# Two heads per instruction and a Softplus in the stick-breaking attention, another issue order in the dilated attention

## The chip, the cores and the metric

The kernel runs on one core of a Trainium2 chip. The time is the device time of one execution in microseconds; lower is better. The kernel before takes 3784.22 us (median of three runs, 3783.95 to 3786.22). TensorE's clock has two levels, 1.2 and 2.4 GHz; the profile gives the granted clock as a share of the upper one.

## The reference, cut to what matters

One program computes two blocks, one after the other, for 256 tokens of width 1024 in float32. The first block (gated linear attention, latent attention, convolution, feed-forward, two layers) is not touched. The second block has two layers. Each is a norm, an attention, a feed-forward part and a gated addition. The attention of layer 0 is stick-breaking attention over 16 heads of 64, that of layer 1 is dilated attention over 8 heads with three dilations.

```python
def stick_breaking_attention(x, w_in, w_out):
    ...
        z = jnp.einsum('bqhd,bkhd->bhqk', q[:, t0:L], k[:, :L]).astype(jnp.float32) * scale
        ...
        past = s_idx < t_idx
        log_fail = jnp.where(past, jax.nn.log_sigmoid(-z), 0.0)
        later = lax.cumsum(log_fail, axis=3, reverse=True) - log_fail
        a = jnp.where(past, jnp.exp(jax.nn.log_sigmoid(z) + later), 0.0)
        outs.append(jnp.einsum('bhqk,bkhd->bqhd', a.astype(v.dtype), v[:, :L]))
    ...
def banded_attention(q, k, v, n_back):
    ...
    s = jnp.where(mask[None, :, None], s, -jnp.inf)
    lse = jax.nn.logsumexp(s, axis=-1)
    prob = jnp.exp(s - lse[..., None])
    o = jnp.einsum('nbhqk,nbkhd->nbqhd', prob.astype(v.dtype), v2)
```

log_sigmoid(-z) is minus softplus(z), and the exponent log_sigmoid(z) + later is z minus the sum of softplus(z) over this key and all later past keys. The dilated attention is a softmax over the three dilations' scores together, weighted sums of the values included.

## The kernel before, in words

All activations lie transposed in SBUF, features on the 128 partitions and tokens along the free dimension. Weights stream through a ring of three buffers of 1 MB that SyncE fills. A planner (`Plan`) gives every output tile a PSUM bank in the order in which TensorE will write it (`pl.tiles`, `pl.gemm`; `pl.on` chooses the banks that are taken in turn), and each engine's program waits for counters: `done(t)` (TensorE has written tile t), `freed(t)` (its reader has emptied the bank). `start_tile` waits until the bank's last user has been read. On ScalarE and VectorE every program is a written list, in order.

Stick stage (layer 0 of the second block). Queries, keys (`QK`) and values (`V2`) are ready. For one head the three causal blocks of 128 x 128 (keys in the partitions) lie side by side as 384 columns. Per head h: TensorE writes the logits (`sz`, L1111 and L1112, 64 rows, since a head is 64 wide). ScalarE copies them scaled (L1235), takes Abs and Exp (through `own`, L1242) and Ln (L1235). VectorE (`failures`) adds the positive part (L2243) and multiplies by the mask (L2244). TensorE sums over later keys with a triangular matrix (`sc`, L1124 to L1127). VectorE (`argument`) subtracts (L2253) and takes the minimum with 0 (L2255), ScalarE takes Exp, VectorE (`stick`) multiplies by the mask (L2260). After each second head TensorE multiplies with the values (`so`, L1136 to L1138), and VectorE copies the 128 rows of the pair to the operand of the output projection `b2out0` (L712), which waits for pair k before its k-th step. TensorE issues the logits of head h + 1 before the sums of head h. The buffers are parts of the temporaries `TA` and `TD`.

Dilated stage (layer 1). A unit u is one head and one half of the queries (u odd: both key tiles, so twice the work). TensorE writes the scores of the three dilations (`d.s`, L1160, 6 or 12 matmul records), VectorE adds the mask and takes the maximum (`dmax`, L2289, L2293, L2294), ScalarE takes Exp with the sum (`dexp`), VectorE inverts the sum and scales (L2309, L2310), TensorE transposes (`d.t`, L793, 3 or 6), ScalarE copies the transposes to SBUF, TensorE multiplies with the values (`d.v`, L1179, 6 or 12), VectorE copies the output (`dvalue`, L2301). TensorE's order is scores of u + 1, transposes of u, values of u. ScalarE's is copies of u, Exp of u + 1. VectorE's is maximum of u + 1, scaling of u, output of u - 1. Probabilities and transposes have one buffer each. A float32 matmul shows as two records; a transpose as one. The projection `b2out1` (L712) follows.

## Time and profile before

| | |
|---|---|
| median of the runs | 3784.22 us |
| profiled execution, its own time | 3782.29 us |
| its span | 3780.5 us |
| TensorE busy | 3365.9 us (89%) |
| VectorE busy | 1420.6 us (38%) |
| ScalarE busy | 853.3 us (23%) |
| mean granted clock of TensorE | 0.93 |
| stick stage, first logits to projection | 2725.67 to 2846.91 us |
| dilated stage, first scores to projection | 3328.18 to 3461.53 us |

Engines: PE is TensorE's matmul part, PEld its weight loads, DVE is VectorE, ACT is ScalarE, POOL is GpSimd, SP is SyncE. Times in a timeline or chain are from the span's start. A wait in square brackets is the engine's idle time ahead of the instruction and what ended it. Busy time of overlapping matmuls is counted once.

### The profile page before, as it was taken

Reading aid. Unit: us, or ns where it says so; the run is one execution under the profiler, and the core shown is the slowest. Engines: PE = TensorE matmul, PEld = TensorE weight load, DVE = VectorE, ACT = ScalarE, POOL = GpSimd, SP = SyncE. Lnnn points to the kernel's source line nnn. Section 1 sums busy time; section 2 is a strip of 40 time slices with the busy share of each in tenths; the row PEclk is TensorE's granted clock in tenths of the full one; section 3 lists DMA queues with packets and bytes.
Section 4 is the critical chain, followed back from the end, with each engine's and each line's share of the span. In section 5 each row is a group of like instructions: output and inputs, shape, how many; then the busy total and the mean of one; then the engine's idle time right before and its main releaser. Section 6 shows DMA issues by size and latency. Waiting matters only on the chain.

```text
span 3780.5 us, 34902 instructions
## 1 busy us (share of the span) xinstructions
PE 3365.9 (89%) x14299; PEld 2397.9 (63%) x14299; DVE 1420.6 (38%) x2517; ACT 853.3 (23%) x1476; POOL 150.8 (4%) x125
## 2 busy tenths in 40 slices
PE   6987898999999699989888999898868998977998
PEld 3655544444444588436776678787757887755887
DVE  2267785232211588123579321542032102223102
ACT  4033210132221333013320332211262102112101
POOL 4000000000000244000000000000000000000000
PEclk9988899999999899999989999998958999966999
DMA  5212134323333132222223323344402553301453
GB/s 190 72 51 56 34 112 135 90 68 112 101 104 108 57 100 90 69 65 78 57 66 110 94 83 129 123 142 128 133 1 87 149 154 111 112 28 42 135 155 100
DMA packets 419421, 362.00 MB, mean 96 GB/s; under 512 B 20848, under 2 KB 392612, under 8 KB 419264
## 3 DMA queue, kind: packets, MB, share of 16 engines
q1 hardware_dynamic: 416928, 359.11, 30.8%
q8 instruction: 114, 1.87, 0.2%
q0 software_dynamic: 2336, 0.67, 0.1%
q14 instruction: 43, 0.35, 0.0%
HBM read 358.70 MB, written 1.05 MB: 95 GB/s over the span
## 4 chain that ended last, share of the span: by engine, by line
PE 77%; DVE 14%; ACT 4%; issue 2%; DMA 1%; POOL 1%; DVEq 0%; ACTq 0%; POOLq 0%
PE banks L712 24%; PE banks L770 12%; PE banks L752 12%; PE banks L687 6%; PE banks L734 5%; DVE conv_out L1954 4%; PE banks L786 3%; ACT L1235 2%; PE banks L1014 2%; PE banks L793 1%; PE banks L1005 1%; DVE gla_att L2016 1%; POOL vector_rows L650 1%; PE banks L955 1%; PE banks L938 1%
## 5 line engine op out<-in xcount | busy, mean ns | idle before, releaser
L712 PE MATMUL banks<-operand_a,wring 128*128 128x256 f32 (+1 forms) x3104 | 769.5, 411 | 44.2 <-DVE operand_a L1750 29.1
L712 PEld LDWEIGHTS banks<-operand_a,wring 128*128 128x128 f32 x3104 | 599.2, 193 | 214.0 <-issue 138.2
L1954 DVE SCALAR_TENSOR_TENSOR conv_out<-conv_in,vectors,conv_out 128x512 f32<-128x512 f32 (+1 forms) x464 | 286.8, 618 | 15.2
L770 PE MATMUL banks<-operand_a,wring 128*128 128x512 f32 (+1 forms) x768 | 263.9, 499 | 21.9 <-DMA wring<-in_w_in_dram 12.8
L770 PEld LDWEIGHTS banks<-operand_a,wring 128*128 128x128 f32 x768 | 146.0, 194 | 132.0 <-issue 98.0
L752 PE MATMUL banks<-ffn_h,wring 128*128 128x512 f32 (+1 forms) x704 | 227.4, 486 | 0.0
L752 PE MATMUL banks<-ff_h,wring 128*128 128x256 f32 x1024 | 221.3, 379 | 0.0
L752 PEld LDWEIGHTS banks<-ff_h,wring 128*128 128x128 f32 x1024 | 194.6, 190 | 26.5
L1005 PE MATMUL banks<-operand_a,wring 128*128 128x512 f32 (+1 forms) x512 | 182.9, 514 | 19.4 <-DVE conv_in L1972 19.4
L752 PEld LDWEIGHTS banks<-ffn_h,wring 128*128 128x128 f32 x704 | 133.8, 190 | 92.9 <-issue 83.5
L770 PE MATMUL banks<-operand_b,wring 128*128 128x512 f32 (+1 forms) x512 | 174.0, 497 | 17.0 <-DMA wring<-in_mla_wo_dram 6.0
L734 PE MATMUL banks<-wring,operand_a 128*128 128x256 f32 x832 | 180.3, 379 | 0.5 <-DVE tmp_dve L1837 0.5
L1235 ACT ACT_TABLE_LOAD x137 | 175.8, 1283 | 3.1 <-PEq L2347 0.7
L734 PEld LDWEIGHTS banks<-wring,operand_a 128*128 128x128 f32 x832 | 158.0, 190 | 22.8 <-issue 1.4
L687 PE MATMUL banks<-operand_a_hi,weights_hi 128*128 128x512 f32 x352 | 138.0, 392 | 29.9 <-POOL weights_lo L655 29.9
L655 POOL TENSOR_TENSOR weights_lo<-wring,weights_hi 128x1024 fp32r<-128x1024 f32 x44 | 108.9, 2476 | 1356.3 <-ACT weights_hi L1235 1356.3
L1005 PEld LDWEIGHTS banks<-operand_a,wring 128*128 128x128 f32 x512 | 102.4, 205 | 84.6 <-issue 76.6
L770 PEld LDWEIGHTS banks<-operand_b,wring 128*128 128x128 f32 x512 | 97.2, 193 | 84.6 <-issue 65.6
L687 PE MATMUL banks<-operand_a_lo,weights_hi 128*128 128x512 f32 x352 | 137.7, 391 | 0.0
L687 PE MATMUL banks<-operand_a_hi,weights_lo 128*128 128x512 f32 x352 | 137.7, 391 | 0.0
L1825 DVE SCALAR_TENSOR_TENSOR resid<-resid,tmp_act 128x512 f32<-128x512 f32 (+1 forms) x32 | 17.9, 559 | 283.1 <-ACT tmp_act L1315 283.1
L1787 DVE TENSOR_SCALAR gate_rank<-banks 128x256 f32<-128x256 f32 x10 | 4.2, 425 | 295.2 <-PE banks L786 295.2
(302 smaller groups left out, 4088.1 us busy)
## 6 DMA issues: line engine op xcount, KB each, us to landing
wring<-in_w_in_dram SPq DMA_DIRECT2D x52, 1024.0 KB, 5.3
wring<-in_w_ada_dram SPq DMA_DIRECT2D x48, 1024.0 KB, 6.5
wring<-in_ffn_wup_dram SPq DMA_DIRECT2D x44, 1024.0 KB, 5.1
wring<-in_w_ff_in_dram SPq DMA_DIRECT2D x32, 1024.0 KB, 5.5
wring<-in_w_ff_out_dram SPq DMA_DIRECT2D x32, 1024.0 KB, 5.6
wring<-in_ffn_wdown_dram SPq DMA_DIRECT2D x32, 704.0 KB, 4.5
wring<-in_w_in_dram SPq DMA_DIRECT2D x36, 512.0 KB, 5.2
wring<-in_w_in_dil_dram SPq DMA_DIRECT2D x18, 1024.0 KB, 5.0
```

The source lines that it names most:

```text
L650: pool.dma_start(VS[r % P:r % P + k, r // P, rep * w:rep * w + w], SRC[name][did:did + k, :]).then_inc(ev("rows_in"), 16)
L655: pool.tensor_tensor(WL[:, u % 2, :, :], w, WH[:, u % 2, :, :].bitcast(F32), ALU.subtract).then_inc(ev("w_lo"), 1)
L687: mm = pe.matmul(bank(t, 0, n), w[:, k, :], x[:, k, 0:n], start=first, stop=last)
L712: mm = pe.matmul(bank(t, 0, n), w[:, k, j * P:(j + 1) * P], opnd[:, k, 0:n], start=k == 0, stop=k == kt - 1)
L734: mm = pe.matmul(bank(t, j * 256, j * 256 + 256), AF[:, k, tok * P:(tok + 1) * P], w[:, k, :], start=k == 0, stop=k == KD - 1)
L752: mm = pe.matmul(bank(t, 0, n), w[:, k % per, :], opnd[:, k, 0:n], start=k == 0, stop=k == kt - 1)
L770: mm = pe.matmul(bank(t + j, 0, n), w[:, k, j * P:(j + 1) * P], (AF if gate else opnd)[:, k, 0:n], start=k == 0, stop=k == KD - 1)
L786: mm = pe.matmul(bank(t, 0, n), cn("ones"), src[:, m, 0:n], start=m == m0, stop=m == m1 - 1)
L1005: mm = pe.matmul(bank(t, 0, n), w[:, k, :], AF[:, k, 0:n], start=k == 0, stop=k == KD - 1)
L1014: mm = pe.matmul(bank(t + j, 0, n), w[:, k, j * P:(j + 1) * P], AF[:, k, 0:n], start=k == 0, stop=k == KD - 1)
L1235: act.activation(dst, src, f, **kw).then_inc(*inc)
L1954: own(stt(dst, src, w, dst, ALU.mult, ALU.add))
```

## The change

In the stick stage everything is done for a pair of heads at once, as instructions over 2 x 384 columns. The logits of a pair lie in two neighbouring banks (0 and 1, or 2 and 3), the sums of a pair in banks 4 and 5, the outputs in 6 or 7. VectorE copies the logits, scales them and adds a mask of 0 and -1e30 in one instruction; the mask constants are changed to these values. ScalarE takes one Softplus over the pair; there is no multiplication by a mask, since both Softplus and Exp of the masked entries are 0. TensorE's order is: logits of pairs 0 and 1, then for each p the sums of p, the values of p - 1, the logits of p + 2. ScalarE's is: Softplus of 0, then Softplus of p + 1, Exp of p. VectorE's is: logits of p + 1, argument of p, output of p - 1.

In the dilated stage probabilities and transposes get two buffers each. TensorE issues transposes of u, values of u - 1, scores of u + 2; ScalarE Exp of u + 1, copies of u; VectorE keeps maximum of u + 1, scaling of u, and copies the output of u - 2. The first block is unchanged.

```diff
-    strict = i[:, None] < i[None, :]
-    add("stick", np.concatenate([strict, np.ones((P, P)), strict], 1), 1)
+    future = np.where(i[:, None] < i[None, :], 0.0, NEG)
+    add("stick", np.concatenate([future, np.zeros((P, P)), future], 1), 1)
...
-    PD, PDT, _ = area(t_at, ("dil_probs", [P, 1, 768]), ("dil_probs_t", [P, 1, 768]))
+    ZS, _ = area(td_at - 8192, ("stick_z", [P, 2, 2, 384]))
+    LF, _ = area(td_at, ("stick_failures", [P, 2, 2, 384]))
+    XS, _ = area(t_at, ("stick_arg", [P, 2, 2, 384]))
+    PD, _ = area(t_at, ("dil_probs", [P, 2, 768]))
+    PDT, _ = area(base + KD * 4096, ("dil_probs_t", [P, 2, 768]))
...
+            logit_banks, sum_banks, out_banks = (0, 2), (4,), (6, 7)
...
+    def banks(t, n):
+
+        b = pl.tile_bank[t]
+        return PS[:, b:b + 2, 0:n]
...
```

TensorE, stick stage:

```diff
+                logits(0)
+                logits(1)
+                for p in range(9):
+                    if p < 8:
+                        t = F[f"sc{p}"]
                         start_tile(t)
+                        counter("failures", 1)(0)
+                        cum = banks(t, 384)
+                        for j in range(2):
+                            lf = LF[:, p % 2, j, :]
...
+                    if p:
+                        t = F[f"so{p - 1}"]
+                        start_tile(t)
+                        counter("stick_exp", 1)(0)
...
+                    if p + 2 < 8:
+                        logits(p + 2)
```

TensorE, dilated stage:

```diff
-                dscores(0)
-                for u in range(16):
-                    h, qt = u // 2, u % 2
-                    if u + 1 < 16:
-                        dscores(u + 1)
-                    counter("probs", 1)(0)
-                    for jt in range(qt + 1):
-                        turn(F[f"d.t{u}"] + jt, [PD[:, 0, jt * 384 + g * P:jt * 384 + (g + 1) * P] for g in range(3)])
...
+                dscores(0)
+                dscores(1)
+                for u in range(17):
+                    if u < 16:
+                        counter("probs", 1)(0)
+                        for jt in range(u % 2 + 1):
+                            turn(F[f"d.t{u}"] + jt,
+                                 [PD[:, u % 2, jt * 384 + g * P:jt * 384 + (g + 1) * P] for g in range(3)])
+                    if u:
+                        dvalues(u - 1)
+                    if u + 2 < 16:
+                        dscores(u + 2)
```

ScalarE, stick stage:

```diff
-                        op(z, bank(t, 0, 384), ACT.Copy, free(t), scale=0.125)
-                        act.wait_ge(*freed(t))
-                        own(w, z, ACT.Abs)
-                        own(w, w, ACT.Exp, scale=-1.0)
-                        op(w, w, ACT.Ln, (ev("stick_softplus"), 1), bias=1.0)
...
+                def softplus(p):
+                    act.wait_ge(*freed(F[f"sz{p}"]))
+                    if p >= 2:
+                        act.wait_ge(*done(F[f"sc{p - 2}"]))
+                    op(LF[:, p % 2, :, :], ZS[:, p % 2, :, :], ACT.Softplus, (ev("failures"), 1))
+
+                softplus(0)
+                for p in range(8):
+                    if p + 1 < 8:
+                        softplus(p + 1)
+                    act.wait_ge(ev("stick_arg"), p + 1)
+                    x = XS[:, p % 2, :, :]
+                    op(x, x, ACT.Exp, (ev("stick_exp"), 1))
```

ScalarE, dilated stage:

```diff
                 dexp(0)
                 for u in range(16):
+                    if u < 15:
+                        dexp(u + 1)
                     for jt in range(u % 2 + 1):
                         t = F[f"d.t{u}"] + jt
                         act.wait_ge(*done(t))
...
-                    if u < 15:
-                        dexp(u + 1)
```

VectorE, stick stage:

```diff
+                mask = cn("stick").unsqueeze(1).broadcast_to([P, 2, 384])
+
+                def logits(p):
+
+                    t = F[f"sz{p}"]
                     dve.wait_ge(*done(t))
+                    stt(ZS[:, p % 2, :, :], banks(t, 384), 0.125, mask, ALU.mult, ALU.add).then_inc(*free(t))
...
+                    tt(x, ZS[:, p % 2, :, :], banks(t, 384), ALU.subtract).then_inc(*free(t))
                     dve.wait_ge(*freed(t))
                     ts(x, x, 0.0, None, ALU.min).then_inc(ev("stick_arg"), 1)
...
+                logits(0)
+                for p in range(8):
+                    if p + 1 < 8:
+                        logits(p + 1)
+                    argument(p)
+                    if p:
+                        outputs(p - 1)
+                outputs(7)
```

VectorE, dilated stage:

```diff
-                    ts(PD[:, 0, 0:nk], PD[:, 0, 0:nk], ST[:, u % 2, 3:4], None, ALU.mult).then_inc(ev("probs"), 1)
-                    if u:
-                        dvalue(u - 1)
+                    ts(PD[:, u % 2, 0:nk], PD[:, u % 2, 0:nk], ST[:, u % 2, 3:4], None,
+                       ALU.mult).then_inc(ev("probs"), 1)
+                    if u >= 2:
+                        dvalue(u - 2)
+                dvalue(14)
                 dvalue(15)
```

## Rows read from the trace of the kernel before

**Rows 1.** Windows: busy us (records) of each engine, granted clock, DMA share, GB/s.
```profile
2725.00:2847.00 122.00, 71.47 (x289) 58.71 (x289) 44.36 (x87) 83.14 (x114) 0.00 (x0) 0.52 0.03 9
3328.00:3460.00 132.00, 86.62 (x358) 71.15 (x359) 40.83 (x103) 25.16 (x57) 0.00 (x0) 0.51 0.01 4
```
**Rows 2.** Chain that ended last, 2725 to 2847 us, shares by engine and line.
```profile
by line: ACT L1235 30.4%; ACT tmp_act L1242 13.8%; ACT tmp_act L1235 10.5%; PE banks L1111 7.2%; ACT tmp_dve L1235 6.5%; issue 6.2%; PE banks L1136 5.1%; PE banks L1138 4.8%; DVE tmp_dve L2260 3.7%; PE banks L1137 3.2%; PE banks L1112 2.7%;
```
**Rows 3.** The same chain in order of time (start us, us, what), stick stage.
```profile
2776.80 0.50 ACT tmp_act L1235
...
2791.57 0.50 ACT tmp_act L1235
```
**Rows 4.** Stick stage, ScalarE: groups (busy us, mean ns), then timeline (start, us).
```profile
L1235 ACT ACT_TABLE_LOAD x31 | 39.8, 1283 | 0.6
L1235 ACT ACTIVATE tmp_act<-tmp_act 128x384 f32<-128x384 f32 x16 | 8.4, 522 | 0.2
...
2780.25 1.28 ACT L1235 ACT_TABLE_LOAD   x1
2781.54 0.52 ACT L1235 ACTIVATE tmp_dve<-tmp_dve 128x384 f32<-128x384 f32 x1
```
**Rows 5.** Timeline of TensorE in the middle of the stick stage.
```profile
2789.89 1.22 PE L1111 MATMUL banks<-b_qk 64*128 64x256 f32 x2
...
2791.46 0.79 PE L1124 MATMUL banks<-tmp_dve,late_consts 128*128 128x128 f32 x2
...
2793.47 1.22 PE L1111 MATMUL banks<-b_qk 64*128 64x256 f32 x2
```
**Rows 6.** Timeline of TensorE at the start of the stick stage.
```profile
2725.67 0.71 PE L1111 MATMUL banks<-b_qk 64*128 64x256 f32 x4 [0.89 <-ACT b_v L1235]
...
2726.18 0.42 PE L1112 MATMUL banks<-b_qk 64*128 64x128 f32 x4
...
2732.70 0.77 PE L1124 MATMUL banks<-tmp_dve,late_consts 128*128 128x128 f32 x2 [6.10 <-DVE tmp_dve L2244]
```
**Rows 7.** Timeline of TensorE at the end of the stick stage.
```profile
2844.98 0.66 PE L1136 MATMUL banks<-tmp_dve,b_v 128*64 128x128 f32 x2 [2.28 <-DVE tmp_dve L2260]
...
2846.91 5.34 PE L712 MATMUL banks<-b_operand,wring 128*128 128x256 f32 x18
```
**Rows 8.** Dilated stage: groups of instructions that are 768 wide.
```profile
L2293 DVE TENSOR_REDUCE stats<-tmp_dve 128x1 f32<-128x768 f32 x8 | 7.6, 953 | 0.8
L1235 ACT ACTIVATE dil_probs<-tmp_dve,stats 128x768 f32<-128x768 f32 x8 | 7.4, 926 | 0.0
...
L2310 DVE TENSOR_SCALAR dil_probs<-dil_probs,stats 128x768 f32<-128x768 f32 x8 | 5.0, 621 | 0.3
```
**Rows 9.** Timeline, first block, full clock: matmuls of 128 columns.
```profile
1842.28 1.95 PE L889 MATMUL banks<-gla_e_more 128*128 128x128 f32 x16
```
**Rows 10.** Dilated stage: timeline, and one entry (3374.15) of the chain.
```profile
3333.20 0.90 PE L793 MATMUL banks<-consts,dil_probs 128*128 128x128 f32 x3 [2.79 <-DVE dil_probs L2310]
...
3374.15 1.54 PE banks L793 x6
...
3376.32 2.79 PE L1179 MATMUL banks<-dil_probs_t,b_v 128*64 128x128 f32 x12 [0.63 <-issue]
...
3379.04 2.93 PE L1160 MATMUL banks<-b_qk 64*128 64x128 f32 x12
...
3384.39 0.90 PE L793 MATMUL banks<-consts,dil_probs 128*128 128x128 f32 x3 [2.42 <-DVE dil_probs L2310]
...
3385.87 1.54 PE L1179 MATMUL banks<-dil_probs_t,b_v 128*64 128x128 f32 x6 [0.58 <-ACT dil_probs_t L1235]
```
**Rows 11.** Windows, columns as in rows 1, around and beside the stick stage.
```profile
2728.00:2732.00 4.00, 0.00 (x0) 0.00 (x0) 0.56 (x1) 3.93 (x6) 0.00 (x0) 0.74 0.28 96
2848.00:2852.00 4.00, 4.00 (x17) 3.42 (x16) 0.00 (x0) 0.14 (x1) 0.00 (x0) 0.83 0.00 0
2000.00:2020.00 20.00, 14.45 (x64) 11.83 (x65) 18.64 (x40) 1.89 (x4) 0.00 (x0) 1.00 0.33 105
```

More of the change, by code:

```diff
@@ L319, in branch_phase @@
                     after=ada_slot if name[2:] == "0" and (name != "co0" or h) else lambda: None)
-    def units(tag, n, s_tiles, t_tiles):
-        pl.tiles(f"{tag}.s0", s_tiles(0))
-        for u in range(n):
-            if u + 1 < n:
-                pl.tiles(f"{tag}.s{u + 1}", s_tiles(u + 1))
-            pl.tiles(f"{tag}.t{u}", t_tiles(u))
-            pl.tiles(f"{tag}.v{u}", 1)
     def ada_half(l, b, h):
@@ L1115, in _ @@
-                logits(0)
-                for h in range(16):
-                    if h < 15:
-                        logits(h + 1)
-                    t = F[f"sc{h}"]
-                    start_tile(t)
-                    counter("failures", 1)(0)
-                    lf = TD[:, h % 2, :]
-                    pe.matmul(bank(t, 0, P), cn("tri"), lf[:, 0:P], start=True, stop=True)
-                    pe.matmul(bank(t, P, 256), cn("tri"), lf[:, P:256], start=True, stop=False)
-                    pe.matmul(bank(t, P, 256), cn("ones"), lf[:, 256:384], start=False, stop=True)
-                    pe.matmul(bank(t, 256, 384), cn("tri"), lf[:, 256:384], start=True, stop=True).then_inc(*made(t))
-                    if h % 2:
-                        t = F[f"so{h // 2}"]
-                        start_tile(t)
-                        pe.wait_ge(ev("sticks"), h + 1)
-                        for hh in (h - 1, h):
-                            o = PS[64 * (hh % 2):64 * (hh % 2) + 64, pl.tile_bank[t], :]
-                            at_ = TD[:, 2 + hh % 2, :]
-                            vv = V2[:, :, hh * 64:hh * 64 + 64]
+                    z = banks(t, 384)
@@ L1139, in _ @@
                         mm.then_inc(*made(t))
+                    if p + 2 < 8:
+                        logits(p + 2)
                 cols("b2out0", KD, B2, SEQ, lambda k: pe.wait_ge(*freed(F[f"so{k}"])))
@@ L1677, in _ @@
                         act.wait_ge(*done(t))
-                        if u:
-                            act.wait_ge(*done(F[f"d.v{u - 1}"]))
-                        op(PDT[:, 0, jt * 384:(jt + 1) * 384], bank(t, 0, 384), ACT.Copy, free(t))
-                    if u < 15:
-                        dexp(u + 1)
+                        if u >= 2:
+                            act.wait_ge(*done(F[f"d.v{u - 2}"]))
+                        op(PDT[:, u % 2, jt * 384:(jt + 1) * 384], bank(t, 0, 384), ACT.Copy, free(t))
             post(f"b2out{l}", F[f"mpre{l}"])
@@ L2234, in _ @@
                 dve.wait_ge(ev("angles"), 1)
-                mask = cn("stick")
-                def failures(h):
-                    dve.wait_ge(ev("stick_softplus"), h + 1)
-                    z, w, lf = TA[:, h % 2, 0:384], TA[:, 2 + h % 2, 0:384], TD[:, h % 2, 0:384]
-                    if h >= 2:
-                        dve.wait_ge(*done(F[f"sc{h - 2}"]))
-                    own(stt(lf, z, 0.0, w, ALU.max, ALU.add))
-                    tt(lf, lf, mask, ALU.mult).then_inc(ev("failures"), 1)
@@ L2246, in argument, with logits @@
[L2246 to L2253 removed]
+                mask = cn("stick").unsqueeze(1).broadcast_to([P, 2, 384])
+                def logits(p):
+                    t = F[f"sz{p}"]
+                    dve.wait_ge(*done(t))
+                    stt(ZS[:, p % 2, :, :], banks(t, 384), 0.125, mask, ALU.mult, ALU.add).then_inc(*free(t))
@@ L2254, in argument @@
+                def argument(p):
+                    t = F[f"sc{p}"]
+                    x = XS[:, p % 2, :, :]
+                    dve.wait_ge(*done(t))
+                    if p >= 2:
+                        dve.wait_ge(*done(F[f"so{p - 2}"]))
+                    tt(x, ZS[:, p % 2, :, :], banks(t, 384), ALU.subtract).then_inc(*free(t))
                     dve.wait_ge(*freed(t))
                     ts(x, x, 0.0, None, ALU.min).then_inc(ev("stick_arg"), 1)
-                def stick(h):
-                    x = TD[:, 2 + h % 2, 0:384]
-                    dve.wait_ge(ev("stick_exp"), h + 1)
-                    tt(x, x, mask, ALU.mult).then_inc(ev("sticks"), 1)
-                    if h % 2:
-                        t = F[f"so{h // 2}"]
-                        dve.wait_ge(*done(t))
-                        if h == 1:
-                            dve.wait_ge(*done(pl.last("wout1")))
-                        dve.tensor_copy(B2[:, h // 2, :], bank(t, 0, SEQ)).then_inc(*free(t))
@@ L2268, in _, with outputs @@
-                failures(0)
-                for h in range(16):
-                    argument(h)
-                    if h < 15:
-                        failures(h + 1)
-                    stick(h)
+                def outputs(p):
+                    t = F[f"so{p}"]
+                    dve.wait_ge(*done(t))
+                    if p == 0:
+                        dve.wait_ge(*done(pl.last("wout1")))
+                    dve.tensor_copy(B2[:, p, :], bank(t, 0, SEQ)).then_inc(*free(t))
+                logits(0)
```

78 lines of the change are left out of this document (42 added, 36 removed).

## Prediction

> **What bounds the kernel now.** I read the windows view first, since the change touches only two stretches of the second block: the stick-breaking attention (2725.7 to 2846.9 us) and the dilated attention (3328.2 to 3461 us). The reader should see TensorE busy for 71 of 122 us in the one and 87 of 132 us in the other, at a mean granted clock of 0.52 and 0.51, and DMA at 1 to 3% [rows 1]. So neither stretch is bound by weights, and in both TensorE waits for somebody. The chain of waits says for whom. In the stick stretch the three ScalarE entries at its head hold over half of the path, with the ACT lines L1235 and L1242 in front [rows 2]; the groups by form show why: 31 table loads of 1283 ns, more than all of one kind of activation (16 of 522 ns) [rows 4]. The pattern repeats every pair of heads: from one first copy on ScalarE to the same copy one pair later is 2791.57 - 2776.80 = 14.77 us [rows 3], eight times. In the dilated stretch the path alternates between TensorE and VectorE: the transposes (L793) waited 2.42 us for the scaled probabilities, and the values (L1179) waited for the ScalarE copy of the transposes [rows 10].
>
> **Stick stage: ScalarE.** A head loses the copy out of PSUM, Abs, Exp, Ln and two of its table switches (Exp to Ln and back); a pair of heads now has one Softplus and one Exp, each 768 wide. A 384-wide activation takes 522 ns [rows 4], a 768-wide one with a per-partition bias and a running sum 926 ns [rows 8]; I take 0.9 us. No row shows Softplus. Its table may be in one set with Exp (no loads, below) or in another (a load before every activation, above). From a load's start to the activation behind it is 2781.54 - 2780.25 = 1.29 us [rows 4]. So ScalarE has 1.8 us per pair at the least and 2 x (1.30 + 0.90) = 4.4 us at the most. I take 4.4, since every Exp/Ln alternation of the kernel before has its load. Against the 14.77 us this is the main gain.
>
> Here the Trainium skill speaks against the change. "ScalarE: Activation LUTs" (What ACT_TABLE_LOAD costs) puts a switch at 1283 ns for the load and 1380 ns for a drain, 2.66 us in all, and its table of sets says to batch by set, which an order that alternates Softplus and Exp does not do. The trace agrees on the load and disagrees on the drain, since the activation started 1.29 us after the load began. By the page of the Trainium skill ScalarE would have 2 x (2.66 + 0.90) = 7.1 us per pair, by the rows 4.4.
>
> **Stick stage: VectorE.** Per pair it now has the scaled and masked copy of the logits, the subtraction, the minimum and one output copy. A 768-wide reduction took 0.953 us, a 768-wide scalar operation 0.621 us [rows 8]. That is about 1.0 + 1.0 + 0.6 + 0.4 = 3.0 us, beside other work. The multiplications by the mask go. The mask's new constants have the old size, and the buffers that move take no instruction.
>
> **Stick stage: TensorE.** The matmuls are the same, so what counts is the clock and the packing. At half clock the 8 matmul records of one head's sums took 2793.47 - 2791.46 = 2.01 us and the logits of one head 2791.46 - 2789.89 = 1.57 us [rows 5]; the values of a pair took 2846.91 - 2844.98 = 1.93 us [rows 7]. At full clock 16 records of 128 columns took 1.95 us [rows 9], that is 0.112 us from one to the next, and the first two heads' logits, issued back to back on different row groups, took 2726.60 - 2725.67 = 0.93 us together [rows 6]. A pair at full clock is 16 x 0.112 + 0.2 = 2.0 (sums), 1.0 (logits) and half of 1.93, about 1.1 (values): 4.1 us. A pair at half clock is 2 x 1.85 = 3.7, then 1.7 to 3.1 for the logits (packed as at the start, or not), and 1.93: 7.4 to 8.7 us.
>
> Which clock? In the kernel before, TensorE finished its first logits at 2726.6 and had nothing until 2732.7 [rows 6], because ScalarE needed two loads and four activations per head; the granted clock fell inside 2728 to 2732 and stayed at 1.2 GHz to 2849 [rows 1, 11]. With the change the first sums need one copy on VectorE (1.0) and one Softplus (0.9, its load done during the wait), so TensorE idles about 1 us instead of 6, and afterwards it is busy 4.1 of every 4.4 us. Elsewhere 2.4 GHz held through 20 us in which TensorE was busy for 14.45 [rows 11]. I take full clock.
>
> **Stick stage: the sum.** First logits at 2725.67, + 0.93, + 1.05 (VectorE), + 0.95 (ScalarE) = first sums at 2728.6. The first Exp runs at about 2732.3, after its subtraction, and ends at 2733.2; with a load the third Softplus ends at 2735.4. Five more pairs at 4.4 us bring the last Softplus to 2757.4. Then sums 2.0, subtraction and minimum 1.7, Exp 0.9, values 1.1: 2763.1. Before it was 2846.91 [rows 7]: 83.8 us saved. The output projection also starts at full clock; before it ran at half to about 2849.3 (0.83 of 2848 to 2852) [rows 11], which gives back 1.2 us. Together 85 us. If no loads are needed TensorE's 4.1 us bounds the pair, 2 us less; if TensorE's starts cost 0.3 us each as at half clock, 5 us more. Nothing stands behind the waits that were added: SyncE has the next weights in the ring already, and the single pair of banks for the sums is free 1.0 us after a sum, while TensorE has 2.1 us of other work.
>
> **Dilated stage.** The change issues the scores of unit u + 2 after the values of unit u - 1, and doubles the probabilities and their transposes. But VectorE's order is unchanged: maximum of u + 1, then scaling of u. The transposes of u wait for that scaling, and so for the scores of u + 1, which TensorE still issues right in front of those transposes. The loop scores, maximum, scaling, transposes, values stays serial; "two ahead" moves TensorE's issue only. What goes is the wait between transposes and values. Before, 6 transposes began at 3374.15 and the values at 3376.32: 2.17 us; 3 began at 3384.39 and the values at 3385.87: 1.48 us. Twelve values took 3379.04 - 3376.32 = 2.72 us to the next group, 0.16 more than 12 x 0.213 [rows 10]. With other values ready, transposes take 6 x 0.213 + 0.16 = 1.44 and 3 x 0.213 + 0.16 = 0.80. Saved 0.73 and 0.68, over 16 units 11 us. The copies and the Exp that change places on ScalarE are hidden by VectorE and by the values in between (about 1 us each); without that cover each copy costs its 0.5 us again, 12 us in all, and the gain is gone. I take the clock to stay low here: the hole of 2.79 us before the first transposes is unchanged, the clock fell around it, and it stayed at half speed for the stretch (mean 0.51) [rows 1, 10].
>
> **The sum.** 85 + 11 = 96 us off the profiled execution's 3782.3 us (span 3780.5) gives 3686. The median of the runs is 1.9 us higher: 3784.2 - 96 = 3688 us.
>
> **Rivals.**
> 1. TensorE stays at 1.2 GHz through the stick stage (against: the hole shrinks from 6 us to 1; for: it was never raised in this stage, though TensorE was busy for 71 of 122 us). A pair is then 7.4 to 8.7 us, 3.0 to 4.3 more than above, over some 7.5 pairs 23 to 32 us, and the projection starts slowly again, 1 us: 3712 to 3721.
> 2. A switch here costs twice the 1.30 us of the loads seen, as if the engine had to empty first. ScalarE then bounds with 2 x (2.6 + 0.9) = 7.0 us per pair, 2.6 us more in each of 7: 3706. This is the drain that the Trainium skill states in "ScalarE: Activation LUTs" (What ACT_TABLE_LOAD costs).
> 3. The dilated stage gives nothing back, since the freed wait reappears in front of the scaling: 3699.
> 4. The dilated stage really overlaps, so that TensorE's 87 us of work plus starts bound it: about 42 us instead of 11, 3657. Against it stands VectorE's order.
> 5. Slower: Softplus is a costly function. It enters once per pair on the chain of ScalarE. With 12 us gained elsewhere, the kernel gets slower by 0.2% (8 us) once 8 pairs lose 20 us, that is at a pair of 17.3 us: a Softplus of 17.3 - 2.6 - 0.9 = 13.8 us, fifteen times any activation of this width. At that point the time is 3792 us, and Softplus replaces Abs, Exp and Ln on the path of every pair (L1242 and L1235 above). Nothing in the trace is like it.
>
> **How the numbers follow.** Forecast 0.69 (its own range 3682 to 3697), rival 1 0.13, rival 2 0.05, rival 3 0.06, rival 4 0.03, rival 5 0.02 for slower, and 0.02 for a Softplus or a stall just big enough to leave the time as it was. The range reaches from 3676, below the no-load case, to 3716, into rival 1. About 0.2% is what a measurement of this kernel can tell from no change. Faster has 0.96, within 0.2% 0.02, slower 0.02.
>
> **What would show it.** In the profile after: table loads in the stick stretch (about 16, or 1 to 2), the granted clock there at 1.00, the pair's period near 4.4 us with ScalarE busy nearly throughout, the projection L712 starting 37 us after the first logits; in the dilated stretch the transposes still waiting over 2 us for VectorE's scaling, the values not waiting for ScalarE, a length of 122 us. A clock of 0.5 in the stick stretch, a Softplus over 1 us, or scores that run under VectorE's maximum would make it wrong.

## The result, and the profile after

The changed kernel takes 3672.2 us (median, 3667.6 to 3677.2) against 3785.2 us (3784.0 to 3787.7) in the same comparison: ratio 0.9701, 95% interval 0.9684 to 0.9718, or 113 us less. The forecast was 96 us less, 3688 us, with 3676 as the lower end of its range. The direction and the larger part were right, and the time lies 4 us below the range.

Three stretches of the profile after, in the windows view (columns as in rows 1). The first two are the stick stage and the dilated stage, each from the first matmul on its scores to the first of its output projection. The third is the first 4 us of the last projection.

```profile
2733.10:2770.10 37.00, 31.68 (x288) 27.85 (x288) 21.91 (x31) 31.27 (x30) 0.00 (x0) 1.00 0.09 29
...
3250.30:3359.20 108.90, 73.00 (x360) 60.45 (x360) 41.21 (x104) 26.60 (x57) 0.00 (x0) 0.69 0.02 5
...
3359.00:3363.00 4.00, 3.73 (x17) 3.34 (x18) 0.00 (x0) 0.66 (x3) 0.00 (x0) 1.00 0.00 0
```

The same cuts of the kernel before:

```profile
2725.70:2846.90 121.20, 71.34 (x288) 58.56 (x288) 44.36 (x87) 82.72 (x113) 0.00 (x0) 0.52 0.03 9
...
3328.20:3461.50 133.30, 87.44 (x360) 71.53 (x361) 41.13 (x104) 24.95 (x57) 0.00 (x0) 0.51 0.01 4
...
3461.00:3465.00 4.00, 3.47 (x8) 2.86 (x9) 0.17 (x1) 0.00 (x0) 0.00 (x0) 0.50 0.00 0
3465.00:3469.00 4.00, 4.00 (x15) 3.28 (x14) 0.00 (x0) 1.32 (x4) 0.00 (x0) 0.73 0.00 0
```

The stick stage went from 121.2 to 37.0 us at a granted clock of 1.00, 84 us less. The dilated stage went from 133.3 to 109.0 us, 24.4 less. In both kernels it has the same 360 matmul records, so the row splits the gain: TensorE's idle time fell from 45.9 to 35.9 us (10.0 less) and its busy time from 87.4 to 73.0 us (14.4 less). Nearly all of the second is a faster clock for the same matmuls; about 1 us of it is that two groups with no wait between them now overlap at their ends. The projection behind it no longer starts at half clock, which shortens the rest of the kernel by 2.8 us. The stretch between the two stages gave 1.2. The profiled spans differ by 105 us and the medians by 113, mainly because the untouched first block ended 7.5 us later in this execution (last section).

The dilated stage by groups of one shape (busy us, mean ns, idle us before them and who ended it), first after, then before:

```profile
L1196 PE MATMUL banks<-dil_probs_t,b_v 128*64 128x128 f32 x144 | 31.6, 398 | 0.0
L1183 PE MATMUL banks<-b_qk 64*128 64x128 f32 x144 | 25.1, 329 | 0.9 <-ACT b_v L1264 0.9
L809 PE MATMUL banks<-consts,dil_probs 128*128 128x128 f32 x72 | 18.4, 410 | 35.3 <-DVE dil_probs L2332 35.3
```

```profile
L1179 PE MATMUL banks<-dil_probs_t,b_v 128*64 128x128 f32 x144 | 34.7, 425 | 9.7 <-issue 5.0 <-ACT dil_probs_t L1235 4.6
L1160 PE MATMUL banks<-b_qk 64*128 64x128 f32 x144 | 34.2, 415 | 0.9 <-ACT b_v L1235 0.9
L793 PE MATMUL banks<-consts,dil_probs 128*128 128x128 f32 x72 | 19.5, 431 | 35.5 <-DVE dil_probs L2310 35.5
```

Two readings: the wait in front of the values went from 9.7 us to nothing, and the wait of the transposes for VectorE's scaling stayed at 35 us. "Two ahead" hides nothing more behind VectorE; what went is one wait, and the same matmuls became shorter.

### The profile page after: what moved, and what is told of

Read it like the earlier page. It is cut to its first block, busy times and chain, and to the rows that moved or that the text cites. A ratio compares the mean times of both kernels' runs of the same rounds, so it can differ in the third digit from the quotient of the medians.

```text
span 3675.4 us, 34722 instructions
## 1 busy us (share of the span) xinstructions
PE 3315.4 (90%) x14299; PEld 2356.7 (64%) x14299; DVE 1397.7 (38%) x2461; ACT 804.3 (22%) x1393; POOL 151.0 (4%) x125
## 4 chain that ended last, share of the span: by engine, by line
PE 80%; DVE 13%; issue 2%; ACT 2%; DMA 1%; POOL 1%; DVEq 0%; ACTq 0%; POOLq 0%
PE banks L728 24%; PE banks L786 13%; PE banks L768 12%; PE banks L703 7%; PE banks L750 5%; DVE conv_out L1980 4%; PE banks L802 3%; PE banks L1021 2%; PE banks L1030 2%; PE banks L809 1%; POOL vector_rows L666 1%; PE banks L971 1%; PE banks L1057 1%; DVE gla_att L2042 1%; PE banks L954 1%
## 5 line engine op out<-in xcount | busy, mean ns | idle before, releaser
L768 PEld LDWEIGHTS banks<-ffn_h,wring 128*128 128x128 f32 x704 | 133.8, 190 | 92.9 <-issue 83.5
L671 POOL TENSOR_TENSOR weights_lo<-wring,weights_hi 128x1024 fp32r<-128x1024 f32 x44 | 108.9, 2476 | 1363.1 <-ACT weights_hi L1264 1363.1
```

Of the source, the lines that this page charges most:

```text
L671: pool.tensor_tensor(WL[:, u % 2, :, :], w, WH[:, u % 2, :, :].bitcast(F32), ALU.subtract).then_inc(ev("w_lo"), 1)
L768: mm = pe.matmul(bank(t, 0, n), w[:, k % per, :], opnd[:, k, 0:n], start=k == 0, stop=k == kt - 1)
```

## The experiments

All were compared with the kernel before on the same chip, at 3785.2 to 3785.5 us. Lengths of a stage run from its first scores to its projection, in the profiled execution.

### The two halves alone

The first kernel is the changed one with the old loop, buffers and orders of all engines in the dilated stage (its core is shown); the second is the kernel before with the new ones.

```diff
-    PD, _ = area(t_at, ("dil_probs", [P, 2, 768]))
-    PDT, _ = area(base + KD * 4096, ("dil_probs_t", [P, 2, 768]))
+    PD, PDT, _ = area(t_at, ("dil_probs", [P, 1, 768]), ("dil_probs_t", [P, 1, 768]))
...
+                for u in range(16):
                     h, qt = u // 2, u % 2
+                    if u + 1 < 16:
+                        dscores(u + 1)
+                    counter("probs", 1)(0)
...
```

> The stick stage of the kernel after, the dilated stage exactly as before. Clock theory and its rival alike: stick stage 37 us (2733.14 to 2770.17 in the kernel after), dilated stage 133 us as before at a mean granted clock of 0.51, total 3785 - 85 = 3700 us. If the changed stick stage also helped the dilated stage (another phase of the clock), the dilated stage is shorter than 130 us here.

> The dilated stage of the kernel after, the stick stage as before. If the 24.4 us of the dilated stage (133.3 to 109.0) belong to its own new order: dilated stage 109 us at a mean granted clock near 0.7, total 3785 - 27 = 3758 us. If they hang on the stick stage: 122 us at a clock of 0.51, total 3774 us.

Measured: the stick half 3697.6 us (ratio 0.9765, 0.9748 to 0.9781), 87.7 less; the dilated half 3758.6 us (0.9930, 0.9915 to 0.9944), 26.7 less. Together 114.4 against the whole change's 113: they add up. The stick stage took 37.0 us in the one and 121.2 in the other, the dilated stage 133.8 and 108.9. So the missed term is the dilated half's own, and owes nothing to the faster stage ahead of it.

### The removed wait put back

```diff
+                    if u < 16:
+                        for jt in range(u % 2 + 1):
+                            pe.wait_ge(*freed(F[f"d.t{u}"] + jt))
                     if u:
                         dvalues(u - 1)
```

TensorE waits for ScalarE's copies of unit u again before it goes on to the values of u - 1; buffers and order stay as changed.

> The kernel after, except that TensorE waits for ScalarE's copies of the transposes of u before the values of u - 1. This puts back a gap of about 0.6 us between transposes and values, 16 times, 10 us at constant clock. Clock theory (the gain beyond 11 us is granted clock, which comes with transposes, values and scores following each other without a gap): the clock falls back to about 0.51, the dilated stage takes 131 us or more, the projection starts at half clock, total 3699 us. Rival (all of the gain is waits and buffers): the stage takes 109 + 10 = 119 us, total 3682 us.

Measured: 3693.1 us (0.9759, 0.9744 to 0.9773); the stage took 128.4 us, 19.4 more than in the changed kernel. The windows view of its dilated stage:

```profile
3245.80:3374.10 128.30, 82.60 (x360) 67.87 (x360) 41.23 (x104) 26.61 (x57) 0.00 (x0) 0.56 0.01 5
```

TensorE's idle time rose from 35.9 to 45.7 us, the 10 us that were put back. Its busy time for the same records rose by 9.6 us as well (about 1 us of that is the overlap at the ends, lost again). So 10 us of waiting cost 19 us, and the granted clock (0.56 for 0.69) carries most of the other half. The result lies between the two expectations, nearer to the clock theory. The clock did not fall to the 0.51 of the old loop: 5 us of busy time stay, for which this pair of runs shows no cause.

### Only work added to the old loop

The stick half alone (dilated stage 133.8 us, clock 0.51), with 8 matmuls per unit that nobody reads, between the next scores and the wait for the probabilities. They go into bank 7, which the plan keeps free by giving the stage's tiles banks 0 to 6 only:

```diff
                     if u + 1 < 16:
                         dscores(u + 1)
+                    for _ in range(8):
+                        pe.matmul(PS[:, 7, 0:P], cn("ones"), cn("ident"), start=True, stop=True)
                     counter("probs", 1)(0)
```

> The kernel with the new stick stage and the old dilated stage, in which TensorE gets eight matmuls of 128 columns (16 records, result read by nobody, in a bank that the stage leaves free) between the scores of u + 1 and the transposes of u, where it waited 2.2 to 2.4 us. Order and waits stay those of before, work is only added. Clock theory (the granted clock of this stage follows what TensorE does, and it alone is worth a large part): once the clock is up, the pair takes 17.06 us less half of its 9.6 us of matmuls, about 12.5 us, the stage about 103 us instead of 133.8 at a clock near 1.0, total 3697 - 30 - 3 = 3664 us. Rival (the clock is not moved by work that is put in, or is not what the stage is short of): the added records stick out of the holes by 16 x 0.213 - 2.3 = 1.1 us per unit at half clock, the stage takes 150 us, total 3715 us.

Measured: 3660.7 us (0.9668, 0.9654 to 0.9683), 37 us faster than the same kernel without the additions; the stage took 98.1 us. Its windows row, TensorE's timeline over one unit (start, duration, what, idle before it), and the values as a group:

```profile
3244.90:3343.00 98.10, 82.19 (x617) 71.35 (x617) 41.13 (x104) 24.13 (x57) 0.00 (x0) 0.98 0.02 6
```

```profile
3295.23 1.60 PE L1185 MATMUL banks<-b_qk 64*128 64x128 f32 x12
3296.76 2.05 PE L1195 MATMUL banks<-consts 128*128 128x128 f32 x16
3299.25 0.55 PE L811 MATMUL banks<-consts,dil_probs 128*128 128x128 f32 x3 [0.44 <-DVE dil_probs L2330]
3300.38 0.87 PE L1206 MATMUL banks<-dil_probs_t,b_v 128*64 128x128 f32 x6 [0.58 <-ACT dil_probs_t L1262]
```

```profile
L1206 PE MATMUL banks<-dil_probs_t,b_v 128*64 128x128 f32 x144 | 18.9, 277 | 10.1 <-ACT dil_probs_t L1262 10.1
```

Sixteen unread groups of 2.05 us (L1195) fill the old wait for the scaling. TensorE's idle time drops from 46 to 16 us, the clock is 0.98, and the real matmuls take little more than half the time: 82.2 us less 16 x 2.05 us leaves 49 us for what took 87.4 us. The added work hid inside the wait; what it brought is the clock. This is the plainest proof in the case. Orders and waits are the old ones, the values still wait 10.1 us for ScalarE's copies (9.7 before), and 36 us went from the stage. So the clock can be up without transposes, values and scores following each other without a gap.

### The same dilated work in two other orders

TensorE takes the values of u - 1 before the transposes of u (in the plan too):

```diff
+                    if u:
+                        dvalues(u - 1)
                     if u < 16:
                         counter("probs", 1)(0)
...
-                    if u:
-                        dvalues(u - 1)
```

> The kernel after with TensorE's order values of u - 1, transposes of u, scores of u + 2, and VectorE's order as it is. The values then run inside the hole in which TensorE waits for maximum and scaling. The serial loop is scores, maximum, scaling, transposes. At half clock TensorE bounds, 11.4 us per pair, 95 us in all, total 3658 us. At full clock 2.0 + 4.6 + 1.2 = 8 us per pair, 68 us in all, total 3630 us. If it is the gapless run of transposes, values and scores that raises the clock, it stays near 0.5 here; if it is the share of time in which TensorE is busy, it goes up.

VectorE takes the scaling of u + 1 ahead of the maximum of u + 2:

```diff
+                dmax(0)
+                dmax(1)
+                dscale(0)
+                for u in range(16):
+                    if u + 1 < 16:
+                        dscale(u + 1)
+                    if u + 2 < 16:
+                        dmax(u + 2)
+                    if u:
+                        dvalue(u - 1)
```

> The kernel after with VectorE's order in the dilated stage changed: the scaling of u + 1 comes ahead of the maximum of u + 2, so that the transposes of u + 1 no longer wait for the scores of u + 2. Theory that VectorE's order is what keeps the stage serial: TensorE no longer waits 2.2 to 2.4 us per unit; bound by TensorE at half clock 45 records x 0.213 + 6 starts = 11 us per pair, 95 us in all (total 3658), at full clock 7 us per pair, 60 to 70 us in all (total 3625 to 3635). Rival (the ScalarE copies or the banks are next in line): no shorter than 105 us, total 3668 or more.

Measured: values first 3638.7 us (0.9611, 0.9595 to 0.9627), stage 76.9 us. VectorE's order 3627.6 us (0.9583, 0.9569 to 0.9597), stage 64.9 us. The same cuts as before, first of the values-first kernel, then of the reordered VectorE:

```profile
3242.50:3319.30 76.80, 58.07 (x360) 48.15 (x360) 41.13 (x104) 26.08 (x57) 0.00 (x0) 0.83 0.02 8
```

```profile
3246.80:3311.70 64.90, 54.39 (x361) 45.89 (x361) 41.94 (x104) 24.25 (x57) 0.00 (x0) 0.87 0.03 9
```

Values first leave 18.7 us of idle time; the time lies between what was expected at half and at full clock. In the reordered VectorE, idle time is 10.5 us instead of 35.9 and busy time 54.4 instead of 73.0: the overlap itself brought 25 us and the clock that came with it 19. This is the prediction's rival 4. It did not happen in the change, for the reason that the prediction gave (VectorE's order), and it happens when that order is changed. One unit in its timeline:

```profile
3270.41 0.17 DVE L2328 RECIPROCAL stats<-stats 128x1 f32<-128x1 f32 x1 [0.77 <-ACT dil_probs L1264]
3270.61 0.62 DVE L2329 TENSOR_SCALAR dil_probs<-dil_probs,stats 128x768 f32<-128x768 f32 x1
...
3271.28 0.88 PE L809 MATMUL banks<-consts,dil_probs 128*128 128x128 f32 x6 [1.04 <-DVE dil_probs L2329]
```

These six transposes wait 1.04 us for the scaling, where in the changed kernel six wait 2.22 us, and VectorE now waits 0.77 us for ScalarE's Exp. All the waits of transposes for the scaling sum to 9.8 us in this stage, against 35.3.

### Scores three ahead, and a warm start

With the change's VectorE order, the wait can also go if TensorE issues the scores one unit earlier, so that the maximum finds them ready:

```diff
                 dscores(1)
+                dscores(2)
...
-                    if u + 2 < 16:
-                        dscores(u + 2)
+                    if u + 3 < 16:
+                        dscores(u + 3)
```

> The kernel after with the scores one unit further ahead: scores of 0, 1 and 2 first, then transposes of u, values of u - 1, scores of u + 3. VectorE's and ScalarE's orders stay. Theory (VectorE does maximum of u + 1 before scaling of u, so the scores of u + 1 must not stand right in front of the transposes of u): TensorE's hole of 2.2 to 2.4 us closes, ScalarE's Exp hides behind the next maximum too, VectorE at 6.2 to 6.5 us per pair bounds, stage 55 to 62 us with a start at half clock, total 3672 - 50 = 3622 us, some us under the order with early scaling (3627.6). Rival (banks or the copies of the transposes are next): stage over 75 us, total over 3640 us.

The second kernel adds 8 unread matmuls once, between the first scores and the first transposes:

```diff
                 dscores(2)
+                for _ in range(8):
+                    pe.matmul(PS[:, 7, 0:P], cn("ones"), cn("ident"), start=True, stop=True)
```

> The same, with eight matmuls (16 records) that nobody reads between the first scores and the first transposes, into a bank the stage leaves free. TensorE waits there 2.8 us, and the clock fell in it. If that hole is what brings the half-clock start (about 10 us of it in the kernel with early scaling), the clock stays at 1.0, and the stage is 3 to 7 us shorter than without them: total 3617 us. Rival (the clock falls anyway, or VectorE bounds so that it doesn't matter): no difference beyond 2 us.

Measured: 3620.9 us (0.9568, 0.9552 to 0.9584), stage 55.6 us; and 3615.4 us (0.9554, 0.9539 to 0.9568), stage 51.1 us. The start of the stage, windows of 4 us, first without and then with the added matmuls:

```profile
3252.00:3256.00 4.00, 4.00 (x19) 3.45 (x18) 3.14 (x9) 1.74 (x5) 0.00 (x0) 0.50 0.00 0
3256.00:3260.00 4.00, 4.00 (x18) 3.12 (x17) 1.92 (x6) 1.52 (x4) 0.00 (x0) 0.50 0.02 6
3260.00:3264.00 4.00, 4.00 (x25) 3.55 (x24) 1.79 (x6) 0.72 (x3) 0.00 (x0) 0.72 0.00 0
```

```profile
3252.00:3256.00 4.00, 3.53 (x29) 3.05 (x28) 3.83 (x11) 2.23 (x5) 0.00 (x0) 1.00 0.00 0
3256.00:3260.00 4.00, 3.88 (x31) 3.13 (x29) 3.72 (x11) 2.80 (x6) 0.00 (x0) 1.00 0.02 6
3260.00:3264.00 4.00, 4.00 (x32) 3.42 (x30) 3.14 (x8) 1.58 (x5) 0.00 (x0) 1.00 0.00 0
```

Without them TensorE works through at half clock for some 11 us after its first hole of 2.46 us; with them the hole is 0.47 us and the clock never falls. The profiled stage is 4.5 us shorter, the medians differ by 5.5 us. It is the shortest of all the runs: 170 us below the kernel before and 57 below the change. What now limits it is TensorE's own work, and not VectorE as was expected:

```profile
3248.50:3299.50 51.00, 48.98 (x376) 41.44 (x376) 40.87 (x104) 25.85 (x57) 0.00 (x0) 1.00 0.04 11
```

It is busy for 49.0 of 51.0 us, at full clock; VectorE for 40.9.

### The stick stage: what Softplus gave, and what the table loads cost

Pairs and the new order, but with the old functions (Abs, Exp, Ln and VectorE's maximum) in place of Softplus; VectorE's list gets that operation and takes the logits two pairs ahead:

```diff
-                    op(LF[:, p % 2, :, :], ZS[:, p % 2, :, :], ACT.Softplus, (ev("failures"), 1))
+                    w = LF[:, p % 2, :, :]
+                    own(w, ZS[:, p % 2, :, :], ACT.Abs)
+                    own(w, w, ACT.Exp, scale=-1.0)
+                    op(w, w, ACT.Ln, (ev("stick_softplus"), 1), bias=1.0)
```

> The kernel after, but Softplus is taken as before: Abs, Exp, Ln on ScalarE over the pair of heads (two table loads more often than none: Exp to Ln and back), then a VectorE operation for the positive part. Pairing and order stay. Theory that most of the gain is the pairing (each instruction and each load does two heads) with the overlap: ScalarE per pair 4 x 0.85 + 2 x 1.3 = 6.0 us against 14.77 before and 4.3 with Softplus; stage 8 + 8 x 6.0 + 3 = 58 us at full clock, total 3672 + 21 = 3693 us. At half clock (the first sums come only after two loads, 6 us in which TensorE idles as before): bound by TensorE, 7.4 us per pair, 70 us, total 3705 us. Rival (Softplus is the main part): the stage stays over 85 us, total over 3720 us.

Softplus in place of the Exp, so that no table changes (the attention's weights are then other numbers, at the same amount of work):

```diff
                     x = XS[:, p % 2, :, :]
-                    op(x, x, ACT.Exp, (ev("stick_exp"), 1))
+                    op(x, x, ACT.Softplus, (ev("stick_exp"), 1))
```

> The kernel after with Softplus in place of the stick stage's Exp, so that no table switches fall inside it; the weights of the attention are then other numbers. ScalarE per pair falls from 4.31 to 1.7 us. Theory that ScalarE with its two loads and TensorE are nearly level: TensorE bounds at 3.9 to 4.1 us per pair, the stage goes from 37.0 to 34 to 36 us, total 3670 us, hardly to be told from 3672. Rival (the loads were still the price of the stage): over 8 us less.

Measured: 3688.2 us (0.9742, 0.9727 to 0.9756), 5 us under the nearer expectation, stick stage 57.1 us at a clock of 0.82; and 3672.9 us (0.9701, 0.9686 to 0.9715), stick stage 34.5 us. ScalarE by groups in the stick stage of the changed kernel, of the one with the old functions, and of the one without switches:

```profile
L1264 ACT ACT_TABLE_LOAD x14 | 18.0, 1283 | 0.2
L1264 ACT ACTIVATE stick_arg<-stick_arg 128x768 f32<-128x768 f32 x8 | 6.7, 844 | 3.3 <-DVE stick_arg L2278 3.2
L1264 ACT ACTIVATE stick_failures<-stick_z 128x768 f32<-128x768 f32 x8 | 6.7, 843 | 1.1 <-DVE stick_z L2267 1.0
```

```profile
L1264 ACT ACT_TABLE_LOAD x15 | 19.2, 1283 | 0.3
...
L1271 ACT ACT_TABLE_LOAD x2 | 2.6, 1283 | 0.0
```

```profile
L1264 ACT ACTIVATE stick_arg<-stick_arg 128x768 f32<-128x768 f32 x8 | 6.8, 844 | 15.1 <-DVE stick_arg L2278 15.1
...
L1264 ACT ACT_TABLE_LOAD x1 | 1.3, 1283 | 0.0
```

Of the stage's 84 us, 64 come without Softplus: from two heads per instruction, the new order, and the copy and the mask in one VectorE operation, which these runs do not separate. Of the 31 loads 14 go with them, because a pair of heads shares its switches. Softplus brings the other 20; in the medians it is 16, since the same dilated stage took 105.8 us in this kernel and 109.0 in the changed one. The loads beside Softplus cost only 2.6 us in all, since without them TensorE's 3.9 us per pair (0.86 of logits, 1.98 of sums, 1.08 of values by its timeline) stands right behind ScalarE's 4.3. In the total, 3672.9 against 3672.2 us, that is not to be seen; the dilated stage was 1.3 us longer in that kernel. The page "ScalarE: Activation LUTs" of the Trainium skill (section Table sets: the hidden batching unit) has Exp and Ln together in one set, with one load for both; the trace disagrees, since with the old functions it shows 17 loads for 8 pairs.

### Does a hole at the start keep the clock down?

Five copies on ScalarE ahead of the first Softplus make TensorE's first wait as long as it was before:

```diff
+                act.wait_ge(*freed(F["sz0"]))
+                for _ in range(5):
+                    own(XS[:, 1, :, :], ZS[:, 0, :, :], ACT.Copy)
                 softplus(0)
```

> The kernel after, with five more copies of 768 on ScalarE (4.3 us) in front of the first Softplus. TensorE then idles about 5.5 us after the first logits instead of 1.4. Theory (the idle start is what took the clock in the kernel before): the clock falls to half at the start of the stage; it comes back once sums and logits follow each other, as in the kernel with the old functions (clock 1.00 again 17 us after the first logits); the stage takes 37 + 4.3 + 4 to 9 us = 45 to 50 us, total 3682 us. Rival 1 (once low, it stays low in this stage): 65 us, total 3700 us. Rival 2 (the clock doesn't fall): 41.4 us, total 3676 us.

Measured: 3680.5 us (0.9724, 0.9709 to 0.9738), stick stage 44.4 us, just under the 45 to 50 expected. Windows of 4 us from the hole on:

```profile
2732.00:2736.00 4.00, 0.00 (x0) 0.00 (x0) 0.45 (x1) 3.85 (x6) 0.00 (x0) 0.73 0.27 96
2736.00:2740.00 4.00, 1.74 (x8) 1.77 (x9) 0.00 (x0) 3.97 (x4) 0.00 (x0) 0.50 0.00 0
2740.00:2744.00 4.00, 4.00 (x20) 3.39 (x20) 1.85 (x3) 0.51 (x2) 0.00 (x0) 0.50 0.01 4
2744.00:2748.00 4.00, 4.00 (x38) 3.55 (x38) 2.64 (x5) 3.94 (x5) 0.00 (x0) 0.99 0.00 0
```

The clock falls in the hole of 7.0 us, which ends at 2738.26, and is back by 2744, within 6 us of work. The hole is 5.6 us longer than in the changed kernel, where 4.3 of copies were meant: the table load of 1.28 us, which ran during TensorE's first logits, now stands behind the copies. Of the 7.4 us that the stage grew, the longer hole is 5.6 and the slow clock the other 1.7. So a single hole as long as the old one of 6.1 us [rows 6] does not keep this stage at half speed. The kernel with the old functions agrees: a first hole of 6.7 us that ends at 2734.0, half clock to 2740, 0.55 to 2744, 1.00 in 2744 to 2748, and 0.90 over the rest of the stage. There ScalarE makes TensorE wait 0.6 to 2.1 us before the sums of every pair. What kept the old stage at 0.52 for 120 us is then likely its waits in every pair, which were more and longer (49.9 us of idle time in all, against 18.4); no run shows this for the stick stage by itself, with only work added to its old loop.

### The changed kernel again

No edit; the same code once more, beside the runs above.

> The kernel after once more, on the chip of the three kernels beside it. If its first profile (span 3675.4) was long only because the untouched first block ended 7.5 us later than in the kernel before, this one has the stick stage at 37.0 us, the dilated stage at 105 to 111 us (its clock follows no fixed pattern from run to run), and a total of 3667 to 3677 us.

Measured: 3673.6 us (0.9707, 0.9692 to 0.9721), stick stage 37.0 us, dilated stage 109.0 us at a clock of 0.69. The dilated gain beyond the 11 us was no accident of one execution.

## Why the prediction was right and where it was wrong

**Stick stage: right, term by term.** Forecast 37.4 us to the projection, measured 37.0. The forecast had 4.4 us per pair, bound by ScalarE. The timeline of the stage after, one Softplus between its two loads and the sums that wait for it:

```profile
2762.22 1.28 ACT L1264 ACT_TABLE_LOAD   x1
...
2763.51 0.84 ACT L1264 ACTIVATE stick_failures<-stick_z 128x768 f32<-128x768 f32 x1
...
2764.37 1.28 ACT L1264 ACT_TABLE_LOAD   x1
...
2764.50 0.46 PE L1143 MATMUL banks<-stick_failures,late_consts 128*128 128x128 f32 x2 [1.04 <-ACT stick_failures L1264]
```

The sums wait 1.04 us for the Softplus, and start 17.24 us after those of four pairs earlier, 4.31 per pair. Both activations took 0.84 us where 0.90 was taken, from load to activation 1.29 us as read [rows 4], and the first hole was 1.37 us where "about 1" stood. Clock 1.00: rival 1 did not happen. The upper end of the choice on Softplus's table (a load before each activation) was the right one, and its cost small.

**Rivals 2 and 5.** The price of a switch was the 1.29 us of the trace, not twice that. An estimate with the Trainium skill's drain ("ScalarE: Activation LUTs", What ACT_TABLE_LOAD costs) is 7 us per pair; the trace disagrees with 4.31. Softplus at 0.84 us is no costly function.

**Dilated stage: the mechanism right, the size wrong.** "The transposes still waiting over 2 us": 2.22 and 2.42 us after, 35.3 us in all. "The values not waiting for ScalarE": nothing instead of 9.7 us. Predicted 1.44 and 0.80 us from transposes to values:

```profile
3317.72 1.54 PE L809 MATMUL banks<-consts,dil_probs 128*128 128x128 f32 x6 [2.22 <-DVE dil_probs L2332]
...
3319.19 1.54 PE L1196 MATMUL banks<-dil_probs_t,b_v 128*64 128x128 f32 x6
...
3324.87 0.90 PE L809 MATMUL banks<-consts,dil_probs 128*128 128x128 f32 x3 [2.42 <-DVE dil_probs L2332]
...
3325.70 2.58 PE L1196 MATMUL banks<-dil_probs_t,b_v 128*64 128x128 f32 x12
```

Measured 1.47 and 0.83 us. Against 2.17 and 1.48 before that is 0.70 and 0.65 less, 10.8 us over 16 units: the 11 us are there. Rival 3 fell with that, and rival 4 did not happen.

**The step that failed** is "I take the clock to stay low here". The term was 11 us and measured 24.4 in the stage and 2.8 in the projection behind it. Of the 24.4, the removed wait is the 10.8 just given, and the other 13.6 are the same records at a mean clock of 0.69 in place of 0.51. With the projection's 2.8 that is the 16 us beyond the term. The reason given, that the hole of 2.79 us before the first transposes was unchanged, was no reason: the runs with a hole at the start show that the clock returns within 6 to 11 us if work follows, and the old loop with unread work runs at 0.98. What held the clock down was the waiting inside the units, and that was just what the change reduced. It was an omission in the range too: the stick stage had its rival on the clock, the dilated stage none, though it sat at 0.51 with the same kind of waits. All the matmuls of the stage at full clock would have been about 38 us less (87.4 to 49 us), so any part of the way up was worth several us, and the range should have gone below 3676 for it. That the loop would flicker instead of rising fully, no row of before could say.

What measure of the waiting decides stays open. TensorE's idle time in the stage was 45.9 us at a clock of 0.51 (before), 45.7 at 0.56 (wait put back), 35.9 at 0.69 (changed), 18.7 at 0.83 (values first), 15.9 at 0.98 (unread work) and 10.5 at 0.87 (VectorE reordered). The last two do not follow that order, and as a share of the stage the idle time hardly moved in the change itself: 34% before, 33% after. Less waiting came with more clock in the large, but no row gives a rule by which the 0.69 could have been forecast.

**The sum.** The stick half was put at 85 us and measured 87.7 (its stage 84.2, the rest small terms behind it that no run separates). The dilated half was put at 11 and measured 26.7. Of the 17 us between forecast and result, 16 are the second.

## What to carry to other kernels

Where a stage runs at half clock and TensorE waits in every turn, price a removed wait twice: once for the wait, and once for what the matmuls that stay would gain by the full clock; give the second a case of its own in the range. Before anything is reordered there, a few matmuls that nobody reads, put into the wait, tell in one run what the clock is worth. And "issued ahead" overlaps only if every engine's order lets it: here another order on VectorE, or scores one unit earlier on TensorE, took a further 44 to 53 us off the stage, about twice the 24 of the change.

## What the runs showed of the hardware that was not expected

**Work that nobody reads made a stage faster.** 256 added matmul records took the dilated stage from 133.8 to 98.1 us, and 16 records at its start were worth 4.5 us.

**The granted clock flickers inside a steady loop.** In the changed kernel's dilated stage, where the same two units repeat, windows of 4 us read:

```profile
3300.00:3304.00 4.00, 1.83 (x12) 1.47 (x10) 1.96 (x6) 0.69 (x2) 0.00 (x0) 0.92 0.00 0
3304.00:3308.00 4.00, 3.94 (x19) 3.29 (x20) 0.19 (x1) 1.00 (x3) 0.00 (x0) 0.57 0.00 0
3308.00:3312.00 4.00, 1.58 (x11) 1.10 (x9) 3.01 (x7) 1.03 (x2) 0.00 (x0) 0.86 0.00 0
```

```profile
3268.00:3272.00 4.00, 4.00 (x18) 3.61 (x18) 0.00 (x0) 0.44 (x1) 0.00 (x0) 0.50 0.00 0
3272.00:3276.00 4.00, 1.78 (x9) 1.21 (x8) 2.14 (x6) 1.20 (x3) 0.00 (x0) 0.50 0.03 6
```

In the first three windows the dense one (3.94 us busy) has the low clock and the sparse one behind it the high. It is not always so: 30 us earlier a dense and a sparse window both have 0.50. The means of 0.56 and 0.69 are mixtures of the two levels, and what sets their places no run shows.

**The flicker repeats.** The expectation of the second run of the changed kernel said that the clock follows no fixed pattern from run to run. Cut into windows of 4 us from the first scores on, the dilated stage has the same clocks within 0.01 in three executions: the changed kernel, the changed kernel again, and the dilated half alone, where the stage lies 84 us later. With the same dilated code, three other kernels have other patterns and lengths: 105.8 us at 0.74 (old functions), 107.0 at 0.73 (hole at the start) and 110.3 at 0.68 (no table switches). These kernels differ only ahead of the stage, and what picks the pattern no run shows. So the 24.4 us of this stage are one value out of 23 to 28 for the same edit.

**The untouched first block is not constant.** It ended between 2725.4 and 2733.1 us over the profiled executions of these kernels, whose code is the same up to there. The latest is the changed kernel's, whose second profile has 2732.7; both profiled executions were the slowest of their four. The timeline shows one of the places, the first line of the changed kernel, the second of the kernel before:

```profile
1086.00 10.19 PE L786 MATMUL banks<-operand_a,wring 128*128 128x512 f32 x16 [4.19 <-DMA wring<-in_w_in_dram]
```

```profile
1083.19 7.13 PE L770 MATMUL banks<-operand_a,wring 128*128 128x512 f32 x16 [2.88 <-DMA wring<-in_w_in_dram]
```

The weights came 1.3 us later after their wait began, and the same 16 matmuls then took 3.1 us longer, at a granted clock of 0.83 in the window from 1080 to 1100 us where the kernel before has 1.00. A profile of one execution carries up to 8 us that lie ahead of the changed stages; lengths of stages, and not spans, are what can be compared.
